# Three first tiles for each feature block in place of two, and re-ordered ScalarE, VectorE and GpSimd queues

## The reference

```
mod = silu(c) @ w_mod[i] + b_mod[i]                    # six vectors, for x and for ctx
hx  = rmsnorm(x, g_pre_mix) * (1 + sc1) + sh1          # the same for ctx
px  = hx @ w_in[i]                                     # 14 tiles of 128 columns
q, k, v -> attention over 768 keys; fourier_mix; hyena_mix (long convolution)
mix = concat(attn, four, hyena) @ w_out[i]             # 8 tiles
x   = x + ga1 * rmsnorm(mix, g_post_mix)
fx  = rmsnorm(x, g_pre_ffn) * (1 + sc2) + sh2
u   = dwconv3(fx @ w_up[i])                            # 2 x 2816 columns = 44 tiles
y   = (silu(gate) * val) @ w_down[i]
x   = x + ga2 * rmsnorm(y, g_post_ffn)
```

## Time and profile before

| | |
|---|---|
| median of 3 runs | 2690.38 us (2687.37 to 2690.76) |
| profiled execution, its own time | 2689.45 us |
| span in the profile | 2687.6 us |
| TensorE matmul busy | 2401.5 us |
| TensorE weight load busy | 1876.5 us |
| VectorE busy | 1320.9 us |
| ScalarE busy | 1080.3 us |
| GpSimd busy | 638.4 us |
| bytes read from HBM | 283.43 MB |

### The profile page before, as it was taken

One profiled execution on the slowest core, in us unless ns is written; L12 is line 12 of the kernel. 1 busy time (PEld: TensorE's weight loads), 2 busy tenths in 40 slices (PEclk: granted clock), 3 DMA queues, 4 the chain that ended last, 5 costly groups with the idle time before them and its releaser, 6 DMA issues.

```text
span 2687.6 us, 31931 instructions
## 1 busy us (share of the span) xinstructions
PE 2401.5 (89%) x12232; PEld 1876.5 (70%) x12232; DVE 1320.9 (49%) x2071; ACT 1080.3 (40%) x1647; POOL 638.4 (24%) x285
## 2 busy tenths in 40 slices
PE   4997977979999999979887889999999998859998
PEld 3875834857888888867564567888867765547776
DVE  3436943134441344225386216525433288529998
ACT  4324621243332233225264035434332256427776
POOL 1220000132222222232200043444444400112223
PEclk8999968979999999979997889999999989979999
DMA  6430041103322232213302232323313311229997
GB/s 228 179 102 6 1 157 48 38 26 103 102 63 63 95 104 77 63 40 116 102 6 110 79 125 71 96 94 102 100 58 101 102 43 49 87 100 338 349 346 268
DMA packets 81039, 291.29 MB, mean 108 GB/s; under 512 B 10713, under 2 KB 13050, under 8 KB 79932
## 3 DMA queue, kind: packets, MB, share of 16 engines
q1 hardware_dynamic: 71952, 251.26, 27.3%
q10 hardware_dynamic: 6348, 28.51, 3.1%
q0 software_dynamic: 2592, 9.48, 0.9%
HBM read 283.43 MB, written 9.48 MB: 109 GB/s over the span
## 4 chain that ended last, share of the span: by engine, by line
PE 71%; DVE 14%; ACT 5%; DMA 3%; POOL 2%; DVEq 2%; issue 2%; ACTq 1%; SPq 0%; POOLq 0%
PE ps L576 36%; PE ps L623 11%; DVE mlo L2287 4%; PE ps L1173 2%; PE ps L680 2%; PE ps L599 2%; DVE stat L1875 2%; DVE ptl L1891 2%; PE ps L1063 2%; POOL x L538 1%; PE ps L1191 1%; DVE pr L1883 1%; PE ps L1014 1%; PE ps L920 1%; DMA wraw<-in_w_all 1%
## 5 line engine op out<-in xcount | busy, mean ns | idle before, releaser
L532 POOL TENSOR_TENSOR wlo<-wraw,whi 128x1024 fp32r<-128x1024 f32 x208 | 502.5, 2418 | 1789.3 <-ACT whi L1213 1129.9
L576 PE MATMUL ps<-hhi,whi 128*128 128x512 f32 x1624 | 593.1, 365 | 9.6 <-POOL wlo L532 7.6
L576 PE MATMUL ps<-hlo,whi 128*128 128x512 f32 x1624 | 586.6, 361 | 0.0
L576 PE MATMUL ps<-hhi,wlo 128*128 128x512 f32 x1624 | 583.4, 359 | 0.0
L576 PEld LDWEIGHTS ps<-hhi,whi 128*128 128x128 f32 x1624 | 308.5, 190 | 80.6 <-issue 27.3
L576 PEld LDWEIGHTS ps<-hhi,wlo 128*128 128x128 f32 x1624 | 307.3, 189 | 48.1
L576 PEld LDWEIGHTS ps<-hlo,whi 128*128 128x128 f32 x1624 | 308.3, 190 | 46.1 <-issue 1.0
L1756 DVE SCALAR_TENSOR_TENSOR up<-ps,cconv,up 128x511 f32<-128x511 f32 (+1 forms) x132 | 83.2, 658 | 282.5 <-ACT up L1504 280.1
L2287 DVE TENSOR_TENSOR mlo<-mraw,mhi 128x1024 fp32r<-128x1024 f32 x147 | 205.7, 1429 | 7.1 <-ACT mhi L1636 7.0
L1220 ACT ACTIVATE whi<-wraw 128x1024 fp32r<-128x1024 f32 x132 | 139.0, 1053 | 127.5 <-PE ps L623 125.9
L623 PE MATMUL ps<-alo,whi 128*128 128x512 f32 (+1 forms) x528 | 188.0, 356 | 0.0
(11 more groups left out here) (335 smaller groups left out, 4226.9 us busy)
## 6 DMA issues: line engine op xcount, KB each, us to landing
wraw<-in_w_all SPq DMA_DIRECT2D x288, 512.0 KB, 3.5
mraw<-in_w_moe SPq DMA_DIRECT2D x168, 512.0 KB, 5.5
mraw_b<-in_w_mod SPq DMA_DIRECT2D x10, 512.0 KB, 15.4
fl<-in_four ACTq DMA_DIRECT2D x2, 2048.0 KB, 8.3
hd<-in_hyf ACTq DMA_DIRECT2D x2, 2048.0 KB, 8.7
hi<-in_hyi ACTq DMA_DIRECT2D x2, 2048.0 KB, 13.7
slot_rows<-in_slot_rows ACTq DMA_DIRECT2D x1, 3612.0 KB, 20.1
xs<-slot_rows POOLq DMA_DIRECT2D x7, 516.0 KB, 6.7
```

Source lines behind the costliest of these rows:

```text
L532: pool.tensor_tensor(wlo[:, slot, :], wraw[:, AT_W[n] % RING, :], whi[:, slot, :].bitcast(F32), ALU.subtract).then_inc(lo_split, 1)
L576: m = pe.matmul(ps[:, bank + b, 0:w], a, r[:, c0:c0 + w], start=k == 0 and q == 0, stop=k == KT - 1 and q == 2)
```

## The change

- `first_tiles` takes as many tiles as it is given widths. Both feed-forwards give it three (in both chunks), and so does layer 1's input projection; layer 0's input projection and the second block's projection stay at two. It waits for the slab of its last tile before the first matmul.
- ScalarE, in the first two tiles of a chunk, cuts the next slab before it evicts the tile, and waits for `cconv` only after the first cut.
- `y` is cleared by GpSimd, behind its additions to `x` after the mix.
- `spread`: VectorE multiplies the identity by the reciprocals, in two halves (`rdiag`), and TensorE multiplies a matrix of ones by these halves.
- In norms of 768 tokens, VectorE and no longer ScalarE makes the last 256 columns of `nfull`.
- Table loads of ScalarE are placed by small activations: Sqrt in front of the last tile's eviction of the output projection and of the down tiles, Exp at the entry of the attention, Silu at the head of a chunk.
- The cut of slab 2 of the feed-forward stands behind the root of the mix's norm.
- At the entry of the attention, the copy of the values and their low parts stand behind the first two exponentials and minima, and the five transfers' issues in step 4.
- In the second block, slabs 3 and 4 are cut around the root of its norm, and the six issues stand at steps 4, 6 and 8 of the projection.

```diff
@@ GpSimd, behind the additions to x
+                if key[1] == "postmix":
+                    pool.drain()
+                    pool.memset(y[:, :, 0:W], 0.0).then_inc(sem("y_clear"), 1)
@@ first_tiles
-            for z in range(2):
+            for z in range(len(widths)):
                 if not first:
                     pe.wait_ge(acc_free, t + z - 2)
-            slab_ready(n + 1)
+            slab_ready(n + (len(widths) - 1))
@@ spread
-            pe.wait_ge(sem("rinv_ready"), nth(key) + 1)
-            for tt in range(width // P):
-                m = pe.matmul(psf[:, 3072 + tt * P:3072 + tt * P + P], rcol[:, tt:tt + 1].to_broadcast([P, P]), ident[:, :],
-                              start=True, stop=True)
+            rd = rdiag[:, :, :].rearrange("p t n -> p (t n)")
+            half = width // 2
+            for z in range(2):
+                pe.wait_ge(sem("rdiag_ready"), 2 * nth(key) + z + 1)
+                for c0, w, b in segs[width]:
+                    a, e = max(c0, z * half), min(c0 + w, z * half + half)
+                    if a < e:
+                        m = pe.matmul(ps[:, 6 + b, a - c0:e - c0], ones[:, :], rd[:, a:e], start=True, stop=True)
@@ TensorE, input projection and feed-forward
+            together = 3 if L else 2
-            first_tiles(S0, T0, S0, T0, h_rhs, [in_width(L, 0), in_width(L, 1)], L == 0,
+            first_tiles(S0, T0, S0, T0, h_rhs, [in_width(L, s) for s in range(together)], L == 0,
-                if s >= 2:
+                if s >= together:
-                first_tiles(i * FFN_SLABS + F0, i * FFN_TILES + G0, F0, G0, h_rhs, [W, W], False,
+                first_tiles(i * FFN_SLABS + F0, i * FFN_TILES + G0, F0, G0, h_rhs, [W, W, W], False,
@@ ScalarE, norms
+        def load_sqrt():
+            act.activation(consts[:, 15:16], zero_c, ACT.Sqrt)
         def summed_rms(key, width):
-            act.activation(consts[:, 15:16], zero_c, ACT.Sqrt)
@@ ScalarE, second block: unnormed
             act.activation(nrow[:, 0:w], ps[:, bank, 0:w], ACT.Copy).then_inc(sem("sq_ready"), 1)
+            split(B2_SLAB + RING)
             act.wait_ge(sem("sq_used"), (KT + 1) * sq_nth(key) + KT + 1)
             rms(key, width)
+            split(B2_SLAB + RING + 1)
@@ norm_apply
-                for c0, w, b in segs[width]:
-                    act.activation(nfull[:, k % 2, c0:c0 + w], nt[:, k % 2, c0:c0 + w], ACT.Identity,
-                                   bias=bfn(k, b), scale=afn(k, b))
+                act.activation(nfull[:, k % 2, 0:TX], nt[:, k % 2, 0:TX], ACT.Identity, bias=bfn(k, 0), scale=afn(k, 0))
@@ ScalarE, attention
+            act.activation(consts[:, 15:16], zero_c, ACT.Exp)
                 if i < N:
                     exponentials(i)
                     exponentials(i + 1)
+                if i == 0:
+                    values_hi()
+                if i == 4:
+                    filter_tables()
@@ ScalarE, output projection
+                if s == OUT_T - 1:
+                    load_sqrt()
-                split(S0 + IN_T + s + RING)
+                if s < OUT_T - 1:
+                    split(S0 + IN_T + s + RING)
             summed_rms((L, "postmix"), W)
+            split(S0 + IN_T + OUT_T - 1 + RING)
@@ ScalarE, feed-forward
-                act.wait_ge(sem("cconv_ready"), i + (L * CHUNKS + 1))
                 act.wait_ge(sem("ysq_ready"), i * KT + KT * ffn_nth(L))
+                act.activation(consts[:, 15:16], zero_c, ACT.Silu)
...
                         act.wait_ge(slab_done, i * FFN_SLABS + (F0 + s + 1))
+                        if p == 0:
+                            split_in(i, FFN_STEP[L], F0 + s + RING)
+                        if s == 0:
+                            act.wait_ge(sem("cconv_ready"), i + (L * CHUNKS + 1))
                         act.activation(up[:, p % 2, z, 0:W], psf[:, b * 512:b * 512 + W], ACT.Identity,
                                        bias=cconv[:, s, 3:4], scale=cconv[:, s, 1:2]).then_inc(sem("up_mid"), 1)
-                        split_in(i, FFN_STEP[L], F0 + s + RING)
+                        if p:
+                            split_in(i, FFN_STEP[L], F0 + s + RING)
@@ ScalarE, second block's projection
-        act.wait_ge(sem("h_ready"), KT * pre_nth((2, "premix")) + KT)
-        act.dma_start(below[:, :], dram["below"]).then_inc(sem("tables_in"), 16)
-        act.dma_start(namask[:, :], dram["namask"]).then_inc(sem("tables_in"), 16)
...
-        load_table(0)
-        load_table(1)
         for s in range(IN2_T):
             n, t = B2_SLAB + s, B2_TILE + s
-            split(n + RING)
+            if s >= 2:
+                split(n + RING)
@@ VectorE, norms
-            dve.reciprocal(rcol[:, 0:n], rcol[:, 0:n]).then_inc(sem("rinv_ready"), 1)
+            dve.reciprocal(rcol[:, 0:n], rcol[:, 0:n])
+            dve.drain()
+            for z in range(2):
+                t0, h = z * n // 2, n // 2
+                dve.tensor_tensor(rdiag[:, t0:t0 + h, :], ident[:, :].unsqueeze(1).to_broadcast([P, h, P]),
+                                  rcol[:, t0:t0 + h].unsqueeze(2).to_broadcast([P, h, P]), ALU.mult)\
+                   .then_inc(sem("rdiag_ready"), 1)
...
+                    if width == T:
+                        dve.wait_ge(sem("scaled_ready"), KT * pre_nth(key) + k)
+                        dve.tensor_scalar(nfull[:, (k - 1) % 2, TX:T], nt[:, (k - 1) % 2, TX:T], afn(k - 1, 1), bfn(k - 1, 1),
+                                          ALU.mult, ALU.add)
+                        dve.drain()
@@ VectorE, attention and feed-forward
+                if i == 0:
+                    values_lo()
-            dve.memset(y[:, :, 0:W], 0.0)
+                dve.wait_ge(sem("y_clear"), L + 1)
```

More of the change, by code:

```diff
@@ L1381, in _, with filter_tables, values_hi @@
                                    ACT.Copy).then_inc(sem("four_hi"), 1)
-            act.wait_ge(sem("k_roped"), 5 * L + 5)
-            act.dma_start(hw3[0:64, :], dram["hy_w3"][L]).then_inc(sem("hfil_in", L), 16)
-            act.dma_start(hw12[0:33, 0:64], dram["hy_w1"][L]).then_inc(sem("hfil_in", L), 16)
-            act.dma_start(hw12[0:64, 64:128], dram["hy_w2"][L]).then_inc(sem("hfil_in", L), 16)
-            act.dma_start(hdel[:, :], dram["deltas"]).then_inc(sem("hfil_in", L), 16)
-            act.dma_start(hz[0:33, :], dram["z512"]).then_inc(sem("hfil_in", L), 16)
-            act.wait_ge(sem("vt_done"), L + 1)
-            for g in range(2):
-                h = slice(64 * g, 64 * g + 64)
-                m = act.activation(vth[:, g, :, h], psf[:, 2048:2048 + 768].rearrange("p (t n) -> p t n", t=6)[:, :, h],
-                                   ACT.Copy)
-            m.then_inc(sem("pt_hi"), 1)
+            def filter_tables():
+                act.wait_ge(sem("k_roped"), 5 * L + 5)
+                act.dma_start(hw3[0:64, :], dram["hy_w3"][L]).then_inc(sem("hfil_in", L), 16)
+                act.dma_start(hw12[0:33, 0:64], dram["hy_w1"][L]).then_inc(sem("hfil_in", L), 16)
+                act.dma_start(hw12[0:64, 64:128], dram["hy_w2"][L]).then_inc(sem("hfil_in", L), 16)
+                act.dma_start(hdel[:, :], dram["deltas"]).then_inc(sem("hfil_in", L), 16)
+                act.dma_start(hz[0:33, :], dram["z512"]).then_inc(sem("hfil_in", L), 16)
+            def values_hi():
+                act.wait_ge(sem("vt_done"), L + 1)
+                for g in range(2):
+                    h = slice(64 * g, 64 * g + 64)
+                    m = act.activation(vth[:, g, :, h], psf[:, 2048:2048 + 768].rearrange("p (t n) -> p t n", t=6)[:, :, h],
+                                       ACT.Copy)
+                m.then_inc(sem("pt_hi"), 1)
+            act.activation(consts[:, 15:16], zero_c, ACT.Exp)
             steps = attn_steps(L)
@@ L1546, in load_table @@
                 act.dma_start(tab[half, h % 2, :], src).then_inc(sem("tab_in", h % 2), 16)
-        load_table(0)
-        load_table(1)
         for s in range(IN2_T):
             n, t = B2_SLAB + s, B2_TILE + s
-            split(n + RING)
+            if s >= 2:
+                split(n + RING)
+            if s == 4:
+                act.dma_start(below[:, :], dram["below"]).then_inc(sem("tables_in"), 16)
+                act.dma_start(namask[:, :], dram["namask"]).then_inc(sem("tables_in"), 16)
+            if s in (6, 8):
+                load_table(s // 2 - 3)
             if s % 12 < 8:
@@ L1720, in add_squares, with norm_dve @@
             dve.drain()
-        def norm_dve(key, src, width, between=None):
+        def norm_dve(key, src, width, afn, bfn, between=None):
             inverse_rms(key, width)
@@ L1765, in _, with mods @@
         modf = mod[:, :, :, :].rearrange("p l t s -> p (l t s)")
+        def mods(L, a, b):
+            return (lambda k, s: mv[:, L, a, k, s:s + 1]), (lambda k, s: mod[:, L, b * KT + k, s:s + 1])
         def bias(group, bank, part):
@@ L1858, in _, with values_lo @@
                        .then_inc(sem("four_out"), 1)
```

(20 more changed lines are left out.)

8 lines of the change are left out of this document (6 added, 2 removed).

## The result

The changed kernel takes 2704.28 us (median; 2703.53 to 2707.17) against 2690.38: ratio 1.0053, interval 1.0038 to 1.0068. It is slower by 13.9 us. The forecast was 2699.8, range 2686 to 2709: sign and range held, and the size was 4.5 us short. The profiled execution took 2704.28 us, its span is 2702.4.

What follows compares the result with a forecast made beforehand. TensorE was taken as busy for most of the span, first tiles standing between a block-by-block norm and a three-slab ring; terms summed to +7.6, with clock +9.4, on 2690.4: 2699.8 us, range 2686 to 2709.

Steps and rivals of the forecast that it cites:

- Layer 0, chunk 0, booked -0.2: Layer 0's first feed-forward chunk: third tile gains nothing, TensorE waits 5.2 us at the modulation pair as before; -0.2.
- Layer 0, chunk 1, booked 11.2: Layer 0's second feed-forward chunk: waits of 2.6 (slab 2) and 5.2 (pair), slow clock 2.5, sum +10.3; 0.9 more clock.
- Layer 1, chunk 1, booked 6.7: Layer 1's second feed-forward chunk: slab 2 adds 3.6 and slab 3 adds 2.2, +5.8; 0.9 more for clock.
- Rival 3: Every new wait also costs clock, idles of 4.1, 3.6, 2.2 and 2.2 each slowing TensorE: +5, 2704.8 us; chance 0.11.
- Layer 1's projection, booked -0.2: Layer 1's input projection: third tile fills waits for the norm, but both head norms then precede tile 3; -0.2.
- The spread, booked +1.5: Norms: spread needs VectorE's products first, +0.45 in each of 768 tokens, +0.3 in each of 512; four norms +1.5.
- rival 2: Spread priced by instruction: falls from 2.94 to about 1.5, norms gain; 8 us less, 2692; chance 0.09.
- Postmix, booked -0.9 and -1.0: The two postmix norms: slab cut and table load leave the path; -0.9 in layer 0, -1.0 in layer 1.
- Attention, booked +1.8: Attention entry: -1.5 in layer 0, 0 in layer 1; transfer issues in step 4 cost +1.4 and +1.9; together +1.8.
- Clearing y on GpSimd, booked 0: GpSimd behind its last addition: clearing takes at most 7.7 us, over before the next norm's first blocks are due; zero.
- Rival 4: VectorE and GpSimd block each other, a slow clearing delaying the first new 256-column product: +3.5, 2703.3 us; chance 0.04.
- Second block, booked -8.7: Second block's projection: both slabs cut during tile 2, tile 3 waits only for bank 0; -5.6 wait, -3.1 clock, -8.7.

Runs made afterwards that it cites:

- e1: The changed kernel with two first tiles again in both feed-forwards, both chunks: 2674.29 us, ratio 0.9946 against the kernel before.
- e2: The changed kernel, its third first tile in the feed-forwards running 5 (layer 0) or 4 (layer 1) feature blocks behind the other two: 2673.91 us, ratio 0.9945.
- e9: The kernel before with only the third first tile in both feed-forwards added: 2716.99 us, ratio 1.0103.
- e6: As e1, with y cleared by VectorE again, in front of the convolution's weights: 2674.17 us, ratio 0.9947 against the kernel before.
- e3: The changed kernel with four unused float32 matmuls behind the last down tile of every chunk, to fill TensorE's idle: 2701.12 us, ratio 1.0049 against the kernel before.
- e7: As e1, with two first tiles also in layer 1's input projection: 2672.26 us, ratio 0.9936 against the kernel before.
- e5: As e1, with the old spread, TensorE multiplying the broadcast reciprocal by the identity: 2668.77 us, ratio 0.9919 against the kernel before.
- e8: As e1, with the attention's entry as before (transfers, values and low parts in front of the first exponentials): 2672.34 us, ratio 0.9935 against the kernel before.
- e4: The kernel before with only the second block's part of the change: 2681.86 us, ratio 0.9979.

## Why the prediction was right, and where it was short

The mechanism held at each of the feed-forwards' places that it named. The third tile takes away the cover under which the next slab is cut in two parts and its place refilled; the head of chunk 1 waits for slab 2. e1 takes the third tile away and gains 30.0, e2 keeps it, restores the cover and gains 30.4, e9 adds the third tile alone and loses 28.

**Layer 0, chunk 0, booked -0.2.** The pair waits as before: it did, 5.14 us against 5.24, and for the cover, as the step said. The step named the clearing as what the diff takes away; e6 shows that the new order of cut and wait is enough for that, and that with it the clearing's place is worth nothing. What the comparison with the kernel before hides is that 5.1 us were there to be gained (e1).

**Layer 0, chunk 1, booked 11.2 with its 0.9 of clock.** Measured 11.8: 2.6 of idle at the head as said, 5.28 against 5.2 at the pair, 2.5 of slow clock behind it as said, and 1.5 of slow clock at the head for 0.9.

**Layer 1, chunk 1, booked 6.7 with its 0.9 of clock.** Measured 10.6. The idles were 3.58 and 2.37 against 3.6 and 2.2. The term that was mis-sized is the clock: 2.7 in the first tiles and 2.0 behind tile 3's wait, 4.7 where I had 0.9. That is 3.8 of the miss. I had read from layer 0 that 5.24 us of idle slows what follows and 1.5 does not, and put 0.9 between. Rival 3, that every new wait also costs clock, had 0.11 and gave 2704.8; it describes what happened in this trace. But it is no rule: e9 has the same idle of 3.58 us at the same head and no slow clock behind it. e3, where the idle was filled, fits the idle as the cause without showing it. So the term of the sum that failed is shown, the clock, and what decides whether it is paid stays open.

**Layer 1's projection, booked -0.2.** It cost 2.4 from the first block to tile 4. Tile 3 starts 28.1 us after the first block, where my steps gave 27.3, and takes 7.29 instead of 5.49. The missed term is again clock: ScalarE's 3.0 us between the head norms were in the sum, the slow TensorE behind them was not. In e1, with the same code and the same wait at this place, the clock held and the stretch took 33.5 us (1206.20 to 1239.69) against 33.9 in the kernel before: -0.4, close to the -0.2 booked. e7 shows a second thing. With two tiles the norm hands over a block every 2.22 us (two blocks in 4.44, from 1207.28 to 1211.72), against 2.4 in the earlier trace rows, and tile 3 starts 2.0 us sooner than in the kernel before. I had priced the handing of `nfull` to VectorE by the first block only (-0.6), but it shortens every block where the norm is the bound, and the third tile made TensorE the bound there.

**The spread, booked +1.5.** Sign and mechanism were right and rival 2 is out: 2.94 us in both forms. It is 0.64 in a norm of 768 tokens where I had 0.45 and 0.50 in one of 512 where I had 0.3: the drain and the hand-over came on top of the product. For seven norms that makes about 4 us; e5 against e1 gives 3.6 by the traces and 5.5 by the medians, with other differences in both.

**Postmix, booked -0.9 and -1.0.** From the last output tile to the additions, layer 0 took 7.98 us instead of 8.61 and layer 1 5.42 instead of 6.67: -0.6 and -1.3. The Trainium skill (ScalarE: Activation LUTs, What ACT_TABLE_LOAD costs) has a drain of some 1380 ns with each switch of sets. Its 1.4 us more in each postmix would have made -2.3 and -2.4; by that rule the traces disagree: in the kernel after the load of Sqrt in layer 0 takes 1.28 us from 548.21 on, and the next activation begins at 549.50. The measurement decides.

**Attention, booked +1.8.** Between the two kernels, from the Fourier mix to the attention's last tiles, layer 0 stands 0.2 to 0.7 better and layer 1 0.8 worse. The +1.8 was 1.2 to 1.7 too high.

**Clearing y on GpSimd, booked 0.** Zero. Its timeline in the kernel after, layer 0:

```profile
576.41 5.22 POOL L542 MEMSET y<- 128x6144 f32 x1
```

5.22 us where the small row had made at most 7.7, and 5.18 on VectorE (e6). Rival 4 rested on two rows that it called the same product; they are a multiplication (L2030) and a subtraction (L2033) of the same shape. Its hold-up between VectorE and GpSimd had no place to show: the clearing ends at 581.63, before the norm's first product at 585.69, and e1 and e6 differ by 0.1 us.

**Second block, booked -8.7.** Measured -8.5: the wait -5.6 and the clock -2.9.

**Not foreseen.** Behind tile 4 of the second block the kernel after gained 2.9 us, 2.0 of them from the experts to the end. The kernel before has a stretch of low clock near its end (0.77 on average from 2650 to 2657) which the one after lacks; it is the only difference that I found there. No run tests it.

Together, by the traces' own times, span against span, the sum missed by 14.8 - 9.4 = 5.4: layer 1's chunk 1 +3.9, its projection +2.6, the stages around the second block's start +1.2, layer 1's preffn and chunk 0 +0.7 (again clock: 105.13 us for tile 3 and what follows, against 103.70 in the earlier trace rows), layer 0's chunk 1 +0.6, the attention of layer 1 -1.1, the end -2.9, and +0.4 from the rest. Clock behind new waits is some 7 of this. Rival 3 is the better account of the size in this trace, my sum the one of place. That the total came as near as it did is in part luck: the terms that came out dearer than booked make 9.4 us, and 4.0 us of terms that came out cheaper, 2.9 of them at the end with no known cause, offset a part.

## What to carry to other kernels

When a small ring feeds an engine, count the time from the end of the first consumer to the end of the group: that interval is what hides the cut and the refill of the next slab. Interleaving one more tile doesn't lengthen the work, it shortens this interval; if interleaving is wanted, let the last tile lag until the interval is as long as the refill takes (here with a lag of 5 blocks in layer 0 and of 4 in layer 1). Price a new idle of TensorE of 2 to 6 us at its length plus a range for the slow clock behind it: in these traces it was between nothing and 3.2 us. And where an edit compares as "no change" with the kernel before, ask whether it only took the place of a wait that another edit of the same change had removed. A difference of 2 to 5 us between two versions needs its place in the traces: e7 and e8 against e1 have one in their medians that lies where nothing was changed.

## What the runs showed of the hardware

A short idle of TensorE is followed by a stretch at 1.2 GHz in one trace and not in another. After 5.1 to 6.0 us in front of a feed-forward's modulation pair the pair took 1.93 or 1.94 us instead of 0.99 in all eight cases (kernels before and after, e3, e4, e9). After 3.58 us the granted clock was 0.50 in the kernel after and 1.00 in e9; after 3.06 us it was low in three traces and full in four; after 1.5 us it stayed full in the earlier trace rows, and in e1 it was 0.50 from 880 to 883, behind a stop of 1.56 us. What decides it below 5 us is open.

The same instructions can fall on either side of a change of the clock. In the second block's attention, the stretch from its first scores to the load of a table took 78.3 us in the traces of e1, e2 and e4 and 74.0 to 74.7 in the other eleven, with the same instructions and no relation that I can see to what had been changed. Windows of e1 at that place:

```profile
2134.00:2145.00 11.00, 11.00 (x32) 6.68 (x31) 7.96 (x23) 5.31 (x12) 0.00 (x0) 0.50 0.11 30
2145.00:2156.00 11.00, 11.00 (x31) 6.99 (x29) 5.73 (x14) 4.44 (x11) 0.00 (x0) 0.50 0.05 14
```

The same windows of e7:

```profile
2134.00:2145.00 11.00, 11.00 (x33) 6.68 (x32) 7.98 (x23) 5.30 (x12) 0.00 (x0) 0.50 0.11 28
2145.00:2156.00 11.00, 10.92 (x50) 7.11 (x49) 8.73 (x24) 7.06 (x16) 0.00 (x0) 0.95 0.21 57
```

In both, TensorE is always busy in the first window at 0.50. In e7 it gets 0.95 in the second, in e1 it stays at 0.50. So differences of medians below some 4 us between these kernels (e5, e7 and e8 against e1) can be of this origin, and I rest the small terms on the traces of the stages instead. What sets the side stays open. It need not be chance from run to run: the five runs of e1 lie within 1.4 us of each other, the eleven of e4 within 8.2.
